# Gates built among the last U products of an expert layer, and one tile's value rows summed by ScalarE and GpSimd

## The reference

```python
def one(t):                                   # 128 tokens
    q = (t @ wq).reshape(128, 8, 2, 64)
    s = einsum("thpd,hpnd->thpn", q, sub_keys)
    st, it = top_k(s, 16)                     # 16 of 128 sub-keys, on both sides
    best, pos = top_k(all 16 x 16 sums, 16)   # 16 experts for each of 8 heads
    e = indices of these among 128 * 128 experts
    g = softmax(best)
    act = gelu(einsum("thkd,td->thk", eu[e], t))
    return einsum("thk,thkd->td", g * act, ev[e])
```

## Time and profile before

| | us |
|---|---|
| median of 3 runs | 3444.88 (3440.21 to 3452.67) |
| the profiled execution | 3435.58 |
| its span, first to last instruction | 3433.7 |
| TensorE busy in the span | 3097.3 (90%) |
| VectorE busy | 2327.0 (68%) |
| ScalarE busy | 1200.6 (35%) |
| GpSimd busy | 1045.2 (30%) |

### The profile page before, as it was taken

The page is one execution under the profiler, slowest core; times in us unless marked ns, Lnnn a source line. Parts: engine busy times, 40 slices in busy tenths (PEclk is TensorE's granted clock), DMA queues, the critical chain, the costliest instruction groups (busy, mean ns, idle before and its releaser), DMA issues. The chain is left out here.

```text
span 3433.7 us, 48518 instructions
## 1 busy us (share of the span) xinstructions
PE 3097.3 (90%) x17340; PEld 2538.6 (74%) x17340; DVE 2327.0 (68%) x4415; ACT 1200.6 (35%) x2396; POOL 1045.2 (30%) x712
## 2 busy tenths in 40 slices
PE   9999999999989999299789999903989999999998
PEld 8788889987678888287664444402868999998887
DVE  7554647668746999653985555566774988975555
ACT  5344424544422111013970000002544444445454
POOL 5555118300000443551334544465003930000000
PEclk9999999999989999698559999956999999999999
DMA  7666855532133899896679999984314544445554
GB/s 275 228 238 228 299 181 196 169 129 68 43 104 130 325 341 332 304 361 235 195 220 387 393 370 395 386 270 165 112 55 145 180 160 144 146 160 191 195 192 140
DMA packets 211820, 754.17 MB, mean 220 GB/s; under 512 B 23456, under 2 KB 29216, under 8 KB 211616
## 3 DMA queue, kind: packets, MB, share of 16 engines
q1 hardware_dynamic: 135184, 480.59, 40.0%
q0 software_dynamic: 73728, 268.47, 22.0%
q10 hardware_dynamic: 2704, 2.38, 0.2%
HBM read 748.20 MB, written 1.05 MB: 218 GB/s over the span
## 5 line engine op out<-in xcount | busy, mean ns | idle before, releaser
L275 PE MATMUL bank<-H,ring 128*128 128x256 f32 x2304 | 501.0, 380 | 5.5 <-ACT arena L2433 2.8
L2292 POOL DMA_INDIRECT ring_hi<-in_u_rows,arena x256 | 286.2, 1118 | 714.0 <-DVE arena L2582 378.2
L275 PEld LDWEIGHTS bank<-H,ring 128*128 128x128 f32 x2304 | 438.8, 191 | 66.7 <-ACT arena L2433 3.2
L2354 PE MATMUL bank<-ring,arena 128*128 128x512 f32 x1024 | 442.0, 595 | 0.8 <-DVE arena L2596 0.8
L2496 DVE SCALAR_TENSOR_TENSOR H<-ring_hi,arena,H 128x1024 f32<-128x1024 f32 x254 | 326.1, 1284 | 157.8 <-DMA ring_hi<-in_v_rows,arena 154.2
L290 POOL TENSOR_TENSOR ring_r<-ring,ring_hi_r 128x1024 fp32r<-128x1024 f32 x133 | 321.3, 2417 | 360.9 <-ACT ring_hi_r L284 360.8
L2490 DVE CUSTOM_DVE_ANT_1 ring_hi<-ring_hi,H 128x1024 f32<-128x1024 f32 x256 | 312.1, 1222 | 160.8 <-DMA ring_hi<-in_u_rows,arena 159.7
L2292 POOL DMA_INDIRECT ring_hi<-in_v_rows,arena x256 | 286.3, 1118 | 338.1 <-DVE H L2496 305.8
L2354 PEld LDWEIGHTS bank<-ring,arena 128*128 128x128 f32 x1024 | 195.3, 191 | 246.9 <-issue 245.8
L284 ACT ACTIVATE ring_hi_r<-ring 128x1024 fp32r<-128x1024 f32 x235 | 247.4, 1056 | 297.3 <-PE bank L302 247.7
L2902 ACT ACTIVATE ring_hi_r<-ring 128x1024 fp32r<-128x1024 f32 x260 | 275.4, 1059 | 167.2 <-PE bank L2840 167.2
(11 more groups left out here) (504 smaller groups left out, 6296.5 us busy)
## 6 DMA issues: line engine op xcount, KB each, us to landing
ring<-in_peer_u SPq DMA_DIRECT2D x256, 512.0 KB
ring<-in_peer_v SPq DMA_DIRECT2D x256, 512.0 KB
ring<-in_w_in SPq DMA_DIRECT2D x135, 512.0 KB
arena<-in_ada SPq DMA_DIRECT2D x96, 512.0 KB, 5.5
ring<-in_w_f SPq DMA_DIRECT2D x72, 512.0 KB
ring<-in_w_br SPq DMA_DIRECT2D x24, 512.0 KB
ring<-in_w_out SPq DMA_DIRECT2D x24, 512.0 KB
ring<-in_w_q SPq DMA_DIRECT2D x24, 512.0 KB
```

What stands on the lines that cost most here:

```text
L275: mm = pe.matmul(out_ap, col(n, kt), rhs(kt), start=(kt == 0), stop=(kt == KT - 1))
L2292: pool.indirect_dma_start(G[:, j % NH, :], None, rows, bass.IndirectOffsetOnAxis(ap=idx_u[:, c:c + 1], axis=0)).then_inc(g_in[j % NH], 16)
L2354: mm = pe.matmul(bank[2 * t + e][:, :], S[:, c, t * P:(t + 1) * P], ring[:, (n0 + v0 + c) % NS, e * 512:(e + 1) * 512], start=(c == 0), st ...
```

## The change

The new order of the same phase, in words:

- The gates of quads are built among U products 88 (`G0`) to 127: before product c, `build` runs for the quads with `first_row` c, 1 or 2 of the 64 each time. `gate(q)` now multiplies only the blocks up to `first_row[q]`; the later blocks of these 4 columns get the gate itself, copied by ScalarE (`keep_rest`), and are multiplied when their product is there (`gelu_late` writes the GELU into `late`, `gate_late` multiplies).
- The weighted one-hots are shared: ScalarE makes two of a quad's four, VectorE the two others in `hit_rows`, by one tensor_scalar each. The first two quads' are made before GELU 82.
- The value rows (V) of context tile 0 leave VectorE. GpSimd gathers them into slots 2 and 3, ScalarE multiplies each by its weight (`scale_value`), GpSimd adds it to the output (`add_value`). VectorE's steps are 384: U rows of tile 0, U rows of tile 1, V rows of tile 1. After step 128 they use slots 0 and 1, and from step 214 (`LATE_SLOTS`) on also the space of hotA, hotB and late.
- VectorE does two row steps per product from 88 on (`PER_BLOCK`).

```diff
-                STEPS = TT * 2 * PICKS
-                BEFORE = 178
+                STEPS = 3 * PICKS
+                PER_BLOCK = 2
+                FIRST = PICKS + 4
+                G0 = 88
+                first_row = [G0 + q * (NK - G0) // QUADS for q in range(QUADS)]
...
+                LATE_SLOTS = FIRST + PER_BLOCK * (NK - G0 + 1)
...
+                def slot_of(j):
+                    if j < PICKS:
+                        return j % NH
+                    return j % 2 if j < LATE_SLOTS else (0, 1, 4, 5, 6)[(j - LATE_SLOTS) % 5]
...
+                        def gather_value(i):
+                            if i < 2:
+                                pool.wait_ge(spent, PICKS - 1 + i)
+                            elif i == 2:
+                                pool.wait_ge(scaled, 1)
+                            else:
+                                pool.wait_ge(added, i - 2)
+                            pool.indirect_dma_start(
+                                slots[value_slot(i)], None, v_rows,
+                                bass.IndirectOffsetOnAxis(ap=idx_u[:, i:i + 1], axis=0)).then_inc(g_in[value_slot(i)], 16)
+
+                        def add_value(i):
+                            pool.wait_ge(scaled, i + 1)
+                            if i >= 2:
+                                pool.wait_ge(added, i - 1)
+                            rows = slots[value_slot(i)].rearrange("p (a t) -> p a t", a=4)
+                            pool.tensor_tensor(tokens(0), tokens(0), rows, ALU.add).then_inc(added, 1)
...
-                        for j in range(STEPS):
+                        for j in range(PICKS + 2):
                             gather(j)
+                        for i in range(2):
+                            gather_value(i)
+                        for j in range(PICKS + 2, FIRST + PER_BLOCK):
+                            gather(j)
+                        for i in range(PICKS):
+                            j = FIRST + PER_BLOCK * (i + 1)
+                            for k in range(j, min(j + PER_BLOCK, STEPS)):
+                                gather(k)
+                            if i:
+                                add_value(i)
+                            if i + 2 < PICKS:
+                                gather_value(i + 2)
...
                         for c in range(NK):
+                            for q in quads_at(c):
+                                build(q)
                             up(c)
...
-                        pe.wait_ge(a_t, TT)
-                        for q in range(QUADS):
-                            build(q)
-                        pe.wait_ge(v_g, QUADS)
+                        pe.wait_ge(a_rest, QUADS)
+                        pe.wait_ge(v_late, NK - G0)
...
+                        def scale_value(i):
+                            rows = slots[value_slot(i)].rearrange("p (a t) -> p a t", a=4)
+                            act.wait_ge(g_in[value_slot(i)], value_landed(i))
+                            if i == 0:
+                                act.wait_ge(v_wt, 1)
+                            act.activation(tokens(0) if i == 0 else rows, rows, ACT.Copy,
+                                           scale=share[:, i:i + 1]).then_inc(scaled, 1)
...
+                        def gelu_late(c):
+                            t = 4 * built(c)
+                            act.wait_ge(blocks_done, n0 + u0 + c + 1)
+                            if c >= G0 + 4:
+                                act.wait_ge(v_late, c - G0 - 3)
+                            g = act.activation(late[:, c % 4, 0:t], bank[4 + c % 4][:, 0:t], ACT.Gelu)
+                            if t < T:
+                                g = act.activation(S[:, c, t:], bank[4 + c % 4][:, t:T], ACT.Gelu)
+                            g.then_inc(a_gelu, 1)
+
+                        def keep_rest(q):
+                            act.wait_ge(v_g, q + 1)
+                            f = first_row[q]
+                            act.activation(S[:, f:, 4 * q:4 * q + 4],
+                                           bank[q % 4][:, :].rearrange("p (t k) -> p k t", t=4)[:, f:, :],
+                                           ACT.Copy).then_inc(a_rest, 1)
...
+                        weighted_keys(0)
+                        weighted_keys(1)
+                        for c in range(FREE, G0):
                             gelu(c)
-                        for q in range(QUADS):
-                            weighted_keys(q)
-                        gelu_picks(1)
+                        for c in range(G0, NK):
+                            for q in quads_at(c):
+                                keep_rest(q)
+                                if q + 2 < QUADS:
+                                    weighted_keys(q + 2)
+                            gelu_late(c)
+                            scale_value(c - G0)
+                        for i in range(NK - G0, PICKS):
+                            scale_value(i)
...
+                            for u in (2, 3):
+                                t = 4 * q + u
+                                ins = dve.tensor_scalar(hotB[:, q % 2, u, :], cc("iota"), cols_[:, t:t + 1], wts[:, t:t + 1],
+                                                        ALU.is_equal, ALU.mult)
...
+                        def gate_late(c):
+                            t = 4 * built(c)
+                            dve.wait_ge(a_gelu, c + 1)
+                            dve.wait_ge(a_rest, built(c))
+                            dve.tensor_tensor(S[:, c, 0:t], S[:, c, 0:t], late[:, c % 4, 0:t], ALU.mult).then_inc(v_late, 1)
...
-                        dve.wait_ge(a_gelu, NK)
-                        for q in range(QUADS):
-                            gate(q)
-                            if q + 2 < QUADS:
-                                hit_rows(q + 2)
-                            spend()
+                        for c in range(G0, NK):
+                            for n, q in enumerate(quads_at(c)):
+                                gate(q)
+                                if q + 2 < QUADS:
+                                    hit_rows(q + 2)
+                                if n < PER_BLOCK:
+                                    spend()
+                            if c > G0:
+                                gate_late(c - 1)
+                            while step[0] < FIRST + PER_BLOCK * (c - G0 + 1):
+                                spend()
+                        gate_late(NK - 1)
```

More of the change, by code:

```diff
@@ L2236, in build @@
                 neg = A.take(T)
+                late = A.take(4, T)
                 flat = S.rearrange("p c t -> p (c t)")
@@ L2259, in build, with quads_at, built @@
                 PICKS = PEER_H * TOPK
-                STEPS = TT * 2 * PICKS
-                BEFORE = 178
+                STEPS = 3 * PICKS
[3 more added lines that the diff above has]
+                first_row = [G0 + q * (NK - G0) // QUADS for q in range(QUADS)]
+                def quads_at(c):
+                    return [q for q in range(QUADS) if first_row[q] == c]
+                def built(c):
+                    return sum(f <= c for f in first_row)
@@ L2262, in build @@
                 n0 = used[0]
                 u0, v0 = 16, 16 + NK
+                LATE_SLOTS = FIRST + PER_BLOCK * (NK - G0 + 1)
+                picks = [late[:, 3, 0:PICKS], act_]
+                slots = [G[:, i, :] for i in range(NH)]
+                slots += [hotA.rearrange("p a b c -> p (a b c)"), hotB.rearrange("p a b c -> p (a b c)"),
+                          late.rearrange("p a t -> p (a t)")]
                 def tokens(n):
                     return H[:, 4 * n:4 * n + 4, 0, :]
+                def slot_of(j):
+                    if j < PICKS:
+                        return j % NH
+                    return j % 2 if j < LATE_SLOTS else (0, 1, 4, 5, 6)[(j - LATE_SLOTS) % 5]
@@ L2269, in build, with sharers, landed, value_slot @@
+                def sharers(j):
+                    return [x for x in range(j) if slot_of(x) == slot_of(j)]
+                def landed(j):
+                    return 16 * (len(sharers(j)) + 1)
+                def value_slot(i):
+                    return 2 + i % 2
+                def value_landed(i):
+                    return 16 * (PICKS // NH + i // 2 + 1)
                 with Phase("keys_in", "by_q", "n_normed", "n_high", "xt_ps", "a_xt", "s_ps", "a_s", "v_read", "v_diff", "a_e",
-                           "a_far", "v_idx", "v_found", "t_ps", "a_t", "v_chain", "a_gelu", "a_col", "v_hot",
@@ L2500, in pick_weights @@
                         def pick_weights(n):
+                            w = share[:, n * PICKS:(n + 1) * PICKS]
                             dve.wait_ge(a_act, n + 1)
-                            link(dve.tensor_tensor(act_, act_, share[:, n * PICKS:(n + 1) * PICKS], ALU.mult))
+                            dve.tensor_tensor(w, w, picks[n], ALU.mult).then_inc(v_wt, 1)
+                            dve.wait_ge(v_wt, n + 1)
```

(7 more changed lines are left out.)

79 lines of the change are left out of this document (44 added, 35 removed).

## The result

The changed kernel takes 3500.9 us (median of 4 runs, 3494.5 to 3504.3), the kernel before 3444.5 in the same comparison. The ratio is 1.0167 with a 95% interval of 1.0144 to 1.0191. The profiled execution took 3494.5 us with a span of 3492.6, 58.9 us more than the span before.

The account below looks back on a forecast made before the run. Row work bound the phase's end, VectorE and GpSimd stopping each other. Product 88 at 1471.8, 316 us of products, 634 of iterations and 4 of landing end it at 2425, +57: 3502 us, range 3405 to 3590.

Parts of the forecast that it names:

- Start of product 88: First U product with interleaved gates: from 1469.1 to 1471.8 us, 2.67 us added by weighted keys made ahead.
- The U part: U products 88 to 127 with gates: 7.9 us each, VectorE 5.7 plus add 2.4 less 0.2; 316 us in all.
- 1.6 x 2 x 0.22: VectorE's work per U product on two weighted one-hots a quad, 1.6 quads a product, 0.22 us per tensor_scalar.
- The iteration: GpSimd's three gathers and one add after the U products: 6.42 us alone, 7.2 with collisions, 88 times, 634 us.
- break-even: Mean GpSimd iteration over all 128 at which the change neither gains nor loses: 6.97 us.
- The floor: Shortest GpSimd iteration beside the V products: 6.7 us, three rows at 2.25 us with DMA engines full.
- rival 1: Collisions of VectorE and GpSimd cost little: 3396 us, or 3424 with 7.2 in the first stage; chance 0.25.
- Rival 2: TensorE drops to 1.2 GHz among the U products: 9.8 us a product, +76 on the forecast, 3578 us; chance 0.13.
- Rival 3: ScalarE's scalings wait for rows and hold the GELUs: 8.7 us a product, +32, 3534 us; chance 0.08.
- Rival 4: VectorE holds up only GpSimd's adds, not gathers: 6.85 us an iteration after, 7.4 before, 3452 us; chance 0.12.
- What would show it: Signs expected in the changed profile: clock, V products' start, longer row steps and hit_rows, 7.2 us iterations, 195 us at the end.

Follow-up runs that it names:

- tiny_add: Changed kernel with GpSimd's adds shrunk to 8 numbers in place of 1024, waits and gathers kept: 3357.7 us, ratio to before 0.9752.
- gates2: Changed kernel with all 512 row steps on VectorE, no scaling or GpSimd adds, four row slots, then seven after the gates: 3307.1 us, ratio to before 0.9601.
- one_input: Changed kernel with VectorE's row steps from step 130 on as reductions of the row alone, one SBUF input: 3430.0 us, ratio to before 0.9964.
- before_six: Kernel before with six row slots in place of four after the last build, nothing else changed: 3376.2 us, ratio to before 0.9799.

## Why the prediction was right, and where its errors offset

3502 was forecast and 3500.9 measured, with slower at 0.63. By the prediction's own steps:

- *Start of product 88.* 1471.8 forecast; the first build is at 1475.9. TensorE's wait for the search ends at 1460.16 in the changed kernel and at 1456.01 in the one before, so 4.1 us arise before the part that the change touches. Their cause is open: in the seven other runs with the moved gates the first build starts anywhere from 1473.4 to 1482.3. The keys made ahead cost 2.7 us, as worked out: from there to the next product it is 6.4 us (1466.54), before 3.7 (1459.68).
- *The U part.* 7.9 us a product forecast, 8.25 measured, +14 us. The size was near, the mechanism only half right, and the nearness is in part luck. The prediction summed VectorE and the add, and took the two row slots (7.1 us) as covered. The runs show the other order: two slots alone give 6.84, value rows with adds of 8 numbers 7.55, and the full adds bring the last 0.7. What the collisions lengthen on VectorE is the tensor_scalars, 0.925 us for 0.343, which is 72 us of 330; the waits for landings shrink by 43 in return, and the U part is 28 us longer than in tiny_add. VectorE's 5.7 was too high: it adds up lengths of instructions, and these overlap in the trace, as hit_rows (1655.51 + 0.68) and the tensor_scalars after it (1656.12) do by 0.07 us. Busy time says 5.2 a product (gates2). In the same way the 170 of 173 us in the gate stage are 156 busy. With 5.2 the prediction's own sum, 5.2 + 2.4 - 0.2, gives 7.4 and not 7.9. Inside it the term 1.6 x 2 x 0.22 was too low, since a tensor_scalar of this kernel takes 0.343 alone; the 0.22 was that of a uint32 one.
- *The iteration.* 7.2 us forecast over 88 iterations, (2426.3 - 1806) / 88 = 7.05 measured, with the tail in it. That is 620 us, where the forecast had 634 and 4 for the last two rows: -17. The parts without collisions were nearly as given: 0.94 a gather, 2.36 an add, 0.30 between gathers; around the add the gaps are 0.02 before and 0.51 after, where the sum had 0.30 twice. They come to 6.31 for 6.42. But the collisions are uneven: 7.23 us an iteration beside the V products and 6.36 (178 us, 28 adds) after them. Why they are rarer at the end was not tried. The first is more than the 0.73 us of collisions in the prediction: 1.22 - 0.94 = 0.28 on each of three gathers and 0.07 on the add make 0.9. The second is far less (1.06 to 1.16 us a gather).
- *The errors*, +4, +14 and -17, cancel: the phase ends at 2426.3, forecast 2425. The hit to 1 us is luck. The direction is not: it followed from an iteration above the 6.97 us of break-even, and the mean from the first build to the end is (2426.3 - 1475.9) / 128 = 7.4.
- *The floor.* "6.7 during the V products, three times the 2.25 us that full DMA engines gave a row" is wrong. one_input ran 6.3 and tiny_add 5.9 us an iteration at 399 and 414 GB/s; the 2.25 us came from four slots (before_six). This error would have misled had the forecast rested on rival 1, whose time used that floor.
- *Rivals.* Rival 1 (collisions cost little) is refuted by one_input: those with row steps alone cost 71 us. Rival 2 has its sign in the profile, a mean clock of 0.87 in the U part, but TensorE stood 86 us there waiting for the one-hots of VectorE, and at clock 1.00 (gates2) its work is 5.2 us. VectorE's gates waited only once for a build, 7.5 us, so TensorE did not set the pace. Rival 3 (late scalings) did not come: ScalarE waited 0.2 us for value rows in the U part. Rival 4, with its inference of the Trainium skill, is refuted by the gathers of one_input beside those of the changed kernel.
- *What would show it.* No stage at 0.50: so. V products from about 1788: 1806. Row steps and hit_rows well above 1.28 and 0.684: for the row steps beside the V products so (1.83 to 2.12 us on average), among the U products not (1.236), and for hit_rows not (0.685); the tensor_scalars took their place. Iterations of 7.2 us: 7.23 beside the V products only. 195 us after the last V product: 178.

Open stays how the U part would run with its adds at a place in VectorE's order where only gates run, and how much of its 8.25 us is VectorE's own work; neither was tried by itself.

## What to carry to other kernels

Before work moves from VectorE to GpSimd, look for the pairs that hold each other up. Here GpSimd's adds held VectorE's row steps (two rows from SBUF) and tensor_scalars (a table and two small operands from SBUF), and row steps and hit_rows held GpSimd's gathers. Gates, with one input in PSUM, and reductions of one row were not held (0.676 and 1.221 us at most). A GpSimd queue that also issued the gathers became the bound after the U part with a quarter of VectorE's row steps. Price the buffers that such a move takes away: here two of four row slots were worth 71 us, and more slots for all rows (69 us for two in the kernel before, 93 for three beside the moved gates) were worth more than moving the gates (44). And a DMA share of 0.99 is no proof that transfers are the limit; try one or two more buffers first.

## What the runs showed of the hardware that was not expected

- The mean busy share of the DMA engines beside the V products was 0.99 at 383 GB/s with four row slots, and 1.01 to 1.02 at 409 to 416 GB/s with six or seven. The share alone does not tell the throughput.
- An indirect gather that starts inside a VectorE row step with two SBUF inputs is held for most of the rest of it: 0.87 us of 0.99 for the gather at 2305.38. One that started 0.15 us before a sum was not held and did not lengthen it: the gather at 2307.49 took 0.95 us, and the sum beside it 1.28:

```profile
2307.64 1.28 DVE L2496 SCALAR_TENSOR_TENSOR H<-ring_hi,arena,H 128x1024 f32<-128x1024 f32 x1 [1.26 <-DMA ring_hi<-in_v_rows,arena]
```

- An instruction of 0.34 us can be the one that pays: a tensor_scalar of 128x128 took up to 3.16 us beside adds of 2.36, and a mean of 0.925 was the only sign of it in VectorE's groups.
